# Mixture-of-experts layer: the rows of the last two expert pairs stay on the chip

## The reference

```python
def hier_moe(h, ...):
    # one of 4 groups, then the top 2 of its 8 experts, with weights
    combine = jnp.einsum('tk,tke->te', weights, one_hot(eid, 32))
    y = jnp.zeros_like(t)
    for e in range(32):
        a = jax.nn.silu(t @ w_gate[e]) * (t @ w_up[e])      # 1024 -> 256
        y = y + combine[:, e:e + 1] * (a @ w_down[e])       # 256 -> 1024
    return y
...
ffn = hier_moe(h, ...)
h = layer_norm(DEEPNORM_ALPHA * h + ffn, ln2_g[l], ln2_b[l])
```

## Time and profile before

| | us |
|---|---|
| median of 3 runs | 594.32 |
| the three runs | 593.19, 594.32, 616.23 |
| the profiled execution | 593.69 |
| its span | 592.0 |

### The profile page before, as it was taken

How to read it: one execution, slowest core, us unless ns; L and a number is a source line. 1 busy time by engine, 2 the same in 40 slices (tenths; PEclk the granted TensorE clock), 3 DMA queues, 4 the chain that set the end, 5 groups by cost and what they waited for, 6 DMA issues and landing times.

```text
span 592.0 us, 6141 instructions
## 1 busy us (share of the span) xinstructions
PE 499.4 (84%) x2182; PEld 283.7 (48%) x2182; DVE 229.1 (39%) x554; ACT 149.7 (25%) x311; POOL 161.9 (27%) x159
## 2 busy tenths in 40 slices
PE   5999999999799999999547799999786789777490
PEld 4586675856454556888443333333232333332130
DVE  2101482898789751255740211111111110102287
ACT  3233323522246664012410111111111111011032
POOL 2243332387624762033521011211111110101000
PEclk9999999999899999999757899999799998889875
DMA  9844458103029101990757799999999999998613
GB/s 321 298 50 51 51 164 259 38 1 142 1 92 356 52 1 37 389 389 38 276 222 270 303 396 418 422 417 419 421 421 419 422 419 419 422 420 329 237 78 142
DMA packets 42583, 148.29 MB, mean 251 GB/s; under 512 B 11362, under 2 KB 15970, under 8 KB 30264
## 3 DMA queue, kind: packets, MB, share of 16 engines
q1 hardware_dynamic: 37992, 139.71, 62.5%
q0 software_dynamic: 4464, 8.10, 3.7%
q10 hardware_dynamic: 96, 0.08, 0.0%
HBM read 137.16 MB, written 18.87 MB: 264 GB/s over the span
## 4 chain that ended last, share of the span: by engine, by line
PE 54%; DMA 20%; SPq 9%; DVE 7%; issue 5%; POOL 2%; ACT 2%; POOLq 0%; DVEq 0%; ACTq 0%
PE bank L1295 17%; DMA wgu<-in_w_up_dram 10%; PE bank L1460 8%; PE bank L1400 7%; DMA xe<-h_rows,row_from 6%; SPq L486 6%; PE bank L1268 3%; PE bank L1484 3%; PE bank L1362 3%; PE bank L1340 3%; SPq L489 3%; DMA y_rows<-ye,row_to 2%; PE bank L1315 2%; PE bank L1353 2%; PE bank L1446 1%
## 5 line engine op out<-in xcount | busy, mean ns | idle before, releaser
L1460 PE MATMUL bank<-wgu,xeT 128*64 128x512 f32 x512 | 127.9, 657 | 28.0 <-DMA wgu<-in_w_up_dram 27.2
L1460 PEld LDWEIGHTS bank<-wgu,xeT 128*64 128x64 f32 x512 | 42.6, 151 | 102.3 <-issue 100.1
L705 POOL DMA_INDIRECT y_rows<-ye,row_to x15 | 15.1, 1006 | 189.0 <-PE bank L1446 120.0
L1484 PE MATMUL bank<-wd,actT 128*64 128x512 f32 x256 | 60.7, 617 | 1.4 <-ACT actT L859 1.4
L1129 DVE TENSOR_TENSOR act_row<-bank,sil 128x256 f32<-128x256 f32 x16 | 6.8, 425 | 130.3 <-ACT sil L852 130.3
L607 POOL TENSOR_TENSOR ring_low<-ring,wt_high 128x1024 fp32r<-128x1024 f32 x12 | 28.6, 2384 | 55.4 <-ACT wt_high L732 55.4
L852 ACT ACTIVATE sil<-bank 128x256 f32<-128x256 f32 x16 | 6.1, 384 | 138.7 <-PE bank L1460 138.7
L1484 PEld LDWEIGHTS bank<-wd,actT 128*64 128x64 f32 x256 | 20.6, 142 | 37.6 <-issue 37.6
L1295 PE MATMUL bank<-xT_high,ring_low 128*128 128x512 f32 x128 | 32.7, 397 | 0.0
L1143 DVE COPY xeT<-bank 128x512 f32<-128x512 f32 x16 | 11.1, 692 | 54.6 <-PE bank L1446 54.6
L1340 PE MATMUL bank<-kT,qT 64*128 64x128 f32 (+3 forms) x64 | 26.0, 487 | 5.1 <-DVE nmx L995 4.3
(11 more groups left out here) (202 smaller groups left out, 761.8 us busy)
## 6 DMA issues: line engine op xcount, KB each, us to landing
wgu<-in_w_gate_dram SPq DMA_DIRECT2D x32, 1024.0 KB, 23.2
wgu<-in_w_up_dram SPq DMA_DIRECT2D x32, 1024.0 KB, 27.7
wd<-in_w_down_dram SPq DMA_DIRECT2D x32, 1024.0 KB, 28.5
ring<-in_w_in_dram SPq DMA_DIRECT2D x5, 2048.0 KB, 13.1
wo<-in_w_out_dram SPq DMA_DIRECT2D x2, 2048.0 KB, 7.9
y_rows<-zero SPq DMA_DIRECT2D x1, 4096.0 KB, 21.8
yg<-y_rows SPq DMA_DIRECT2D x8, 512.0 KB, 6.6
bias_rows<-brow SPq DMA_DIRECT2D x1, 2560.0 KB
```

Of the source, the lines that this page charges most:

```text
L1460: ins = pe.matmul(bank[2 + i][half_rows(n), :], xeT[i][:, k, half_rows(n)], wgu[slots[n]][:, :, k, :], start=k == 0, stop=k == KD - 1)
L1484: ins = pe.matmul(bank[4 + c][half_rows(n), :], actT[i][:, m, half_rows(n)], wd[PAIR_SLOTS[p % 3][n]][:, m, 512 * c:512 * c + 512], start= ...
```

## The change

`KEPT` is 2: pairs 14 and 15 are not stored but placed by PE, and the 14 pairs 0 to 13 are stored.

- `ye` becomes two buffers; each waits for the store of the pair two before it, and each has its own semaphore.
- `place_w` is made for both kept pairs: 16 instructions on DVE, directly behind the product of pair 0. Both are transposed on PE (8 transposes) behind pair 0's act transposes, and copied out on ACT in two copies. PE waits for both copies and goes on with `rows(2)`.
- The loads of `yg` stand in SP's queue ahead of the test for full experts, behind the loads of `g2` and `b2`, and wait for the stores up to pair 13.
- `place_rows(t, 14)` for tiles 0 and 1 stands ahead of `gate_up(15)`; all else of the placing stands behind `down(15)`, 12 matmuls. Pair 14's and 15's parts add up in the bank.

```diff
+KEPT = 2
+STORED = PAIRS - KEPT
...
-        ye = at("ye", o, [D])
+        ye = [at(f"ye{i}", o + 4 * KB * i, [D]) for i in range(2)]
...
-        LAST_BANKS = ((0, 1), (2, 3), (6, 7), (4, 5))
+        LAST_BANKS = ((0, 1), (2, 6), (3, 7), (4, 5))
...
+            for i in range(2):
+                sp.wait_ge(y_stored[i], 16 * (STORED // 2))
+            for t in range(NT):
+                for c in range(2):
+                    sp.dma_start(yg[t][c][:, :], y_dram[SEQ * c + P * t:SEQ * c + P * t + P, :]).then_inc(y_gathered[t], 16)
+
             sp.wait_ge(y_ps, 2 * LAST)
             sp.wait_ge(count_ready, 1)
...
-            sp.wait_ge(y_stored, 16 * LAST)
-            for t in range(NT):
-                for c in range(2):
-                    sp.dma_start(yg[t][c][:, :], y_dram[SEQ * c + P * t:SEQ * c + P * t + P, :]).then_inc(y_gathered[t], 16)
...
-            for p in range(LAST):
+            for p in range(STORED):
                 if p + 3 < PAIRS:
                     gather(p + 3)
                 store_y(p)
...
             def y_out(p):
                 act.wait_ge(y_ps, 2 * p + 2)
-                if p:
-                    act.wait_ge(y_stored, 16 * p)
-                act.activation(ye[:, 512:], bank[5][:, :], ACT.Copy).then_inc(y_hi, 1)
+                if p >= 2:
+                    act.wait_ge(y_stored[p % 2], 16 * (p // 2))
+                act.activation(ye[p % 2][:, 512:], bank[5][:, :], ACT.Copy).then_inc(y_hi, 1)
...
+            for q in range(KEPT):
+                act.wait_ge(placeT_ps, q + 1)
+                act.activation(placeT[:, q, :, :], bank[4 + q][:, :].rearrange("p (t s) -> p t s", t=NT), ACT.Copy).then_inc(placeT_ready, 1)
...
             gated(0)
+            for q in range(KEPT):
+                for t in range(NT):
+                    for e in range(2):
+                        ins = dve.tensor_scalar(place_w[:, q, t, e, :], iota_r[:, :], last_rank[:, 0, t, 2 * q + e:2 * q + e + 1],
+                                                last_wt[:, 0, t, 2 * q + e:2 * q + e + 1], ALU.is_equal, ALU.mult)
+                ins.then_inc(place_ready, 1)
...
             transpose_act(0)
+            for q in range(KEPT):
+                pe.wait_ge(place_ready, q + 1)
+                for t in range(NT):
+                    ins = pe.transpose(bank[4 + q][:, P * t:P * t + P], place_w[:, q, t, :, :].rearrange("p n s -> p (n s)"), ident[:, :])
+                ins.then_inc(placeT_ps, 1)
+            pe.wait_ge(placeT_ready, KEPT)
             for p in range(LAST - 1):
                 rows(p + 2)
...
+            def place_rows(t, p):
+
+                for c in range(2):
+                    pe.wait_ge((y_lo, y_hi)[c], p + 1)
+                    ins = pe.matmul(bank[LAST_BANKS[t][c]][:, :], placeT[:, p - STORED, t, :], ye[p % 2][:, 512 * c:512 * c + 512],
+                                    start=p == STORED, stop=p == LAST)
+                    if p == LAST:
+                        ins.then_inc(last_ps, 1)
...
+            for t in range(2):
+                place_rows(t, STORED)
             gate_up(LAST)
             transpose_act(LAST)
             down(LAST)
...
+            for t in range(2):
+                place_rows(t, LAST)
+            for t in range(2, NT):
+                place_rows(t, STORED)
+                place_rows(t, LAST)
```

More of the change, by code:

```diff
@@ L144, in layer_kernel @@
         square = at("square", SLOT + 16 * KB, [D])
-        place_w = at("place_w", SLOT + 20 * KB, [NT, 2, CAP])
-        placeT = at("placeT", SLOT + 22 * KB, [NT, P])
         o_rowsT = at("o_rowsT", 5 * SLOT, [KD, SEQ])
@@ L166, in layer_kernel @@
         hT = [at(f"hT{i}", o + 4 * KB * i, [KD, P]) for i in range(2)]
-        ye = at("ye", o, [D])
+        ye = [at(f"ye{i}", o + 4 * KB * i, [D]) for i in range(2)]
+        place_w = at("place_w", o + 4 * KB, [KEPT, NT, 2, CAP])
         o += 8 * KB
@@ L175, in layer_kernel @@
                    [at("x_again1_0", o + 4 * KB, [D // 2]), at("x_again1_1", o + 10 * KB, [D // 2])]]
+        placeT = at("placeT", o, [KEPT, NT, P])
         sil = [at(f"sil{i}", o + 4 * KB + KB * i, [DE]) for i in range(2)]
@@ L244, in layer_kernel @@
         eps_t = small("eps_t", [1])
-        last_rank, last_wt = at("last_rank", wpool_at, [2, NT, 2]), at("last_wt", wpool_at + 64, [2, NT, 2])
-        row_sum, neg_mean = at("row_sum", wpool_at + 128, [NT, 2]), at("neg_mean", wpool_at + 160, [NT])
-        square_sum, std2, rstd2 = [at(name, wpool_at + 192 + 32 * i, [NT]) for i, name in enumerate(("square_sum", "std2", "rstd2"))]
+        last_rank, last_wt = at("last_rank", wpool_at, [2, NT, 2 * KEPT]), at("last_wt", wpool_at + 128, [2, NT, 2 * KEPT])
+        row_sum, neg_mean = at("row_sum", wpool_at + 256, [NT, 2]), at("neg_mean", wpool_at + 288, [NT])
+        square_sum, std2, rstd2 = [at(name, wpool_at + 320 + 32 * i, [NT]) for i, name in enumerate(("square_sum", "std2", "rstd2"))]
         rank1 = small("rank1", [NT, NE])
@@ L366, in layer_kernel @@
         y_hi = sem("y_hi")
-        y_stored = sem("y_stored")
+        y_stored = [sem(f"y_stored{i}") for i in range(2)]
         y_gathered = [sem(f"y_gathered{t}") for t in range(NT)]
@@ L705, in store_y @@
                 pool.indirect_dma_start(out=y_dram, out_offset=bass.IndirectOffsetOnAxis(ap=row_to[:, p:p + 1], axis=0),
-                                        in_=ye[:, :], in_offset=None,
-                                        bounds_check=2 * SEQ - 1, oob_is_err=False).then_inc(y_stored, 16)
+                                        in_=ye[p % 2][:, :], in_offset=None,
+                                        bounds_check=2 * SEQ - 1, oob_is_err=False).then_inc(y_stored[p % 2], 16)
             for p in range(3):
@@ L899, in _ @@
                         act.activation(o_sil[:, m, :], bank[m][:, :], ACT.Silu).then_inc(o_silu_ready, 1)
-            act.wait_ge(placeT_ps, 1)
-            act.activation(placeT[:, :, :], bank[0][:, :].rearrange("p (t s) -> p t s", t=NT), ACT.Copy).then_inc(placeT_ready, 1)
             silu(LAST)
@@ L1132, in y_out @@
                 dve.wait_ge(y_ps, 2 * p + 1)
-                if p:
-                    dve.wait_ge(y_stored, 16 * p)
-                dve.tensor_copy(ye[:, 0:512], bank[4][:, :]).then_inc(y_lo, 1)
+                if p >= 2:
+                    dve.wait_ge(y_stored[p % 2], 16 * (p // 2))
+                dve.tensor_copy(ye[p % 2][:, 0:512], bank[4][:, :]).then_inc(y_lo, 1)
             def rows_out(p):
@@ L1157, in _ @@
             for c in range(2):
-                link(dve.tensor_tensor(last_rank[:, c, :, :], hot[:, :, c, NE - 2:NE], rk[:, :, c:c + 1].to_broadcast([P, NT, 2]), ALU.mult))
-                link(dve.tensor_tensor(last_wt[:, c, :, :], hot[:, :, c, NE - 2:NE], wt[:, :, c:c + 1].to_broadcast([P, NT, 2]), ALU.mult))
+                link(dve.tensor_tensor(last_rank[:, c, :, :], hot[:, :, c, 2 * STORED:NE], rk[:, :, c:c + 1].to_broadcast([P, NT, 2 * KEPT]), ALU.mult))
+                link(dve.tensor_tensor(last_wt[:, c, :, :], hot[:, :, c, 2 * STORED:NE], wt[:, :, c:c + 1].to_broadcast([P, NT, 2 * KEPT]), ALU.mult))
             link(dve.tensor_tensor(last_rank[:, 0, :, :], last_rank[:, 0, :, :], last_rank[:, 1, :, :], ALU.add))
@@ L1166, in _ @@
                 y_out(p)
[L1168 to L1172, removed]
             y_out(LAST - 1)
@@ L1533, in _ @@
                         ins.then_inc(o_y_ps, 1)
+                pe.wait_ge(o_added, NE * NT + 1)
+            def place_rows(t, p):
[5 more added lines that the diff above has]
+                        ins.then_inc(last_ps, 1)
             pe.wait_ge(xeT_act, PAIRS)
             pe.wait_ge(xeT_dve, PAIRS)
[L1537 to L1540, removed]
+            for t in range(2):
+                place_rows(t, STORED)
             gate_up(LAST)
```

## The result

| | median, us | against the kernel before |
|---|---|---|
| before | 594.4 | |
| after | 596.15 | ratio 1.0037, 95% interval 1.0021 to 1.0053 |

The change makes the kernel 2.2 us slower (1.2 to 3.2), where 1.0 us slower was forecast, 595.3 in a range of 589.0 to 599.0. By the bound of 2% it is no change. Some executions of every version are some 3% longer than the others; they are left out of every ratio here, and out of the medians in the table further down.

A forecast was written before the change was run, and what follows sets the result against it. The stream of expert weights was taken to bound the kernel's expert pairs. 593.7 + 5.0 (start) - 4.0 (tail) = 594.7 us for the profiled execution, 595.3 as a median with 0.6 added; 8-in-10 range 589.0 to 599.0.

The forecast's parts named there:

- The bound: Expert pairs: the weight stream bounds them, DMA share 1.02 over 350 to 532 us; later landings come 5.0 us later.
- Rival 2: Start: the new work costs nothing because the weight stream has unseen slack; 590.3 us; chance 0.11.
- The cost of the start: Start: place_w work delays rows(2), so gate_up(1) ends at 344.5 instead of 339.5; 5.0 us, 3.6 to 6.1.
- the chain up to `rows(2)`: Start: place_w on DVE, transposes on PE and ACT's copy finish at 334.85; only then may rows(2) start.
- I keep the row of before: Start: gate_up(1) priced at its earlier 7.65 us, low clock; 7.09 at the high clock, 8.79 after an idle stretch.
- Three of the signs: gate_up(1) ends at 343 to 346, gate_up(15) starts at 549 to 551, add_stored(0) about 9.1 us behind first yg issue.
- the cover that I counted on: Tail: four placing matmuls, 3.6 us, cost nothing while gate_up(15) waits for weights until 544.83; uncovered, 3.6 us.
- The gain of the tail: Tail: without pair 14's store, yg lands and DVE starts 3.8 us earlier; with 0.4 us possible from clock, 4.0 us taken.
- The backlog: Tail: a few DMA engines carry a backlog from the stream; yg's first pair lands 2.56 us behind b2.
- rival 1: Tail: yg lands as fast as alone, the full 8.0 us arrive; 590.3, or 590.9 as a median; chance 0.22.
- rival 3: Tail: at 1.2 GHz PE is the bound, twelve placing matmuls need 21.4 us, add_last(3) 8 us late; 603.3; chance 0.03.
- rival 4: Tail: something else holds SP's queue until 553, no early yg fetch; cost and 0.4 us of clock remain; 599.9; chance 0.04.

The follow-up runs named there:

- experiment 2: Kernel before with the new start block alone (place_w for two pairs, eight transposes, copies, PE's wait ahead of rows(2)), tail as before: 599.6 us.
- experiment 4: Changed kernel with the loads of g2 and b2 issued behind the eight yg loads instead of ahead: 593.8 us.
- experiment 5: Changed kernel with SP waiting for the landing of g2 and b2 before it issues yg: 598.0 us.
- experiment 6: Kernel before with two ye buffers alone, pair 14 still stored, start unchanged: 591.3 us.
- experiment 7: Kernel before with two ye buffers and g2 and b2 loaded behind yg, pair 14 still stored: 591.6 us.
- experiment 3: Changed kernel with 45 unused filler transposes on PE where it waits at the start: 593.1 us.
- experiment 1: Changed kernel, start repaired: place_w's transposes, copies and PE's wait moved behind gate_up(1), ahead of down(0): 590.4 us, repeated 591.0.
- experiment 8: Changed kernel with both edits: place_w's transposes behind gate_up(1), g2 and b2 loaded behind yg: 587.2 us, repeated 587.1.

## Why the prediction was right, point by point

**The bound.** That the stream of weights bounds the pairs, and that a later `gate_up(1)` is carried whole to the end, was right. Five kernels show it, by how much the issue behind `gate_up(1)` and the start of `gate_up(15)` lie behind the earlier trace rows: start alone 6.4 and 6.5 us, changed 6.8 and 7.4, filler 3.5 and 4.1, start repaired 0.8 and 1.0, two buffers 0.1 and 0.3. Rival 2 had no share in it.

**The cost of the start, 5.0 us with 3.6 to 6.1.** In the profiled execution it was 6.8 us at the issue, outside these bounds. Of the 1.8 us too much, 0.3 are the execution itself, which is that much late from `rows(1)` on; the chain up to `rows(2)` was right (335.19, forecast 334.85). What was mis-sized is the step "I keep the row of before" for `gate_up(1)`: 9.15 us, where I took 7.65 and 8.79 as the upper end. The granted clock was 0.50 to 0.51 from 331 to 341: PE's small pieces of work in between did not bring it back.

But 9.15 us is not the price of the change either. With the same start `gate_up(1)` took 8.66 us in experiment 2, 7.67 in experiment 4 and 8.60 in experiment 5; with the start of before it took 7.65, 7.73 (experiment 6) and 8.68 (experiment 7). From the start of `rows(1)` to the issue behind `gate_up(1)` the four kernels with the new start took 19.6 to 21.1 us, 5.0 to 6.5 more than the 14.6 of before. With the clock kept up, in experiment 3, it was 17.75. By the ratio the start alone cost 5.5 us (4.2 to 6.7), so that 5.0 is not refuted as a mean; what was wrong is that I took one row for a duration that differs by 1.5 us from profile to profile. In the changed kernel the granted clock was 0.50 up to 341 and 1.00 from 341.5 on, in experiment 4, where `gate_up(1)` began 1.3 us later, 0.50 up to 339.5 and 1.00 from 340 on; what sets the moment isn't shown.

Three of the signs that I had named were missed by little for this: `gate_up(1)` ended at 346.2 (343 to 346), `gate_up(15)` started at 552.2 (549 to 551), and `add_stored(0)` came 8.3 us behind the issue of `yg` (9.1).

The 0.6 us between 6.8 and 7.4 are PE's. `gate_up(14)` took 9.54 us where it had taken 8.79, and what follows it on PE came 7.8 us late, up to the placing matmuls. They end at 552.29, where `gate_up(15)` starts, and its row names no wait for weights; so the cover that I counted on was used up to the last. It costs nothing, because DVE waits for `yg` until 561.5.

**The gain of the tail, 4.0 us.** It measured 4.3. The first pair of `yg` was to come 3.8 us earlier, counted without the shift; it came 3.6 us earlier, counted from the issue behind `gate_up(1)`. The remaining 0.7 us are the clock: `down(15)` took 5.62 us and not 6.46, and DVE was the bound, as I had allowed with 0.4. By the ratios the tail gained 4.0 us (2.9 to 5.0) where the start is repaired, in experiment 1.

**The backlog.** The step on which the forecast stood against rival 1 was that `yg` comes one landing, 2.56 us, behind `b2`. In four profiles it did: 558.9 and 561.5 in the changed kernel, 556.2 and 558.9 with the filler, 553.9 and 556.4 with the start repaired, 553.7 and 556.2 with two buffers. Experiment 5 shows that alone the same loads need 5.0 us, and experiment 4 that `g2` and `b2` are part of what they wait for. That what they wait for is the stream itself shows when DVE's first use of `yg` is counted from the issue behind `gate_up(1)`:

| kernel | us from that issue to the first use of `yg` |
|---|---|
| before, start alone | 218.8, 218.8 |
| changed, yg waits for b2 | 217.6 |
| two buffers; the same with g2 and b2 behind yg | 216.5, 216.0 |
| changed; filler; start repaired | 215.2, 215.8, 216.0 |
| changed, g2 and b2 behind yg; both edits, twice | 212.7, 212.7, 212.6 |

What the start costs does not enter it, and with `g2` and `b2` behind it is the same to 0.2 us in three profiles, though `yg` was issued 5.9 to 7.5 us before its use. There the pair lands 2.5 to 2.6 us behind the last down weights of pair 15: 556.3 and 558.8 in experiment 4, 550.7 and 553.3, 550.4 and 552.9 in experiment 8. So the step held more widely than I had put it: `yg` comes one landing behind what stands last ahead of it, `b2` or else these weights. That is read from the traces; no run takes the weights away. That it is a few of the sixteen engines that carry the backlog was read from the DMA share, 0.05 at 552 to 553, and not tried.

**The sum.** 593.7 + 6.8 - 4.3 = 596.2, measured 596.0 in the profiled execution, where 594.7 was forecast. The cost was 1.8 us too small there and the gain 0.3. The total still fell into the range because this was wide: a cost outside its own bounds was not provided for, and the range's lower half was there for rivals 1 and 2, and neither had any part in the outcome. That the miss stayed small is in part luck.

**Rivals 3 and 4** did not come. The last placing matmuls ran 24 records in 10.57 us, 0.88 us for each of twelve, and `add_last` never waited for them; `yg` was issued right behind store 13. The number that I gave for rival 4 is a slip: 594.3 + 5.0 - 0.4 is 598.9 and not 599.9, and lies inside the range that was to stop short of it.

## What to carry to other kernels

A step moved from the end to the beginning isn't moved into free time because the engines look idle there: look for who releases the next transfer, and put the step behind that release. Here it stood one instruction group too early, ahead of a matmul group whose end lets the weight stream go on, and its place alone was worth 6 us. Take a duration that hangs on the clock from more than one profile. And when a wait is taken out of a tail, ask what the next transfer stands behind in its queue: the small loads of two parameter rows took away some 2.7 us of the gain until they were issued last. Where a store still held `yg` back for longer, in experiment 7, the same move gained nothing.

## What the runs showed that I had not expected

- Filler work on an idle engine made the kernel 2.3 us faster (the two intervals just do not meet), because the group behind it, on which the stream hangs, ran at 2.4 GHz, a granted clock of 1.00.
- A load of 512 KB issued at the end of a full stream took 14.7 to 17.4 us to land (`b2`, in seven profiles), while 512 KB of a fetch issued afterwards came every 1.3 us.
- Keeping pair 14 on the chip is worth 4.4 us with `g2` and `b2` behind `yg` (587.2 against 591.6), but only 0.9 with them ahead (590.4 against 591.3), which is not clear of the noise: keeping the pair and moving `g2` and `b2` are worth more together than singly.
